# A hybrid decoder step: the samples' values stored by sample, and their new states made ahead of and between the splits of the third tile

## What is computed

```python
s_new = g_c[None, :, None, None] * s + jnp.einsum('bmhd,bmhe->bhde', kc * zeta[None, :, :, None], vc)
return s_new, o_in + o_cross
```

## Time and profile before

| | |
|---|---|
| median of 3 timed runs | 2126.41 us (2126.33 to 2126.54) |
| the profiled execution | 2127.75 us |
| its span in the profile | 2125.9 us |
| PE busy | 2101.2 us, 99% |
| DVE busy | 1449.2 us, 68% |
| ACT busy | 958.2 us, 45% |
| HBM traffic | 196 GB/s over the span |

### The profile page before, as it was taken

The page is one execution under the profiler, slowest core; times in us unless marked ns, Lnnn a source line. Parts: engine busy times, 40 slices in busy tenths (PEclk is TensorE's granted clock), DMA queues, the critical chain, the costliest instruction groups (busy, mean ns, idle before and its releaser), DMA issues.

```text
span 2125.9 us, 46489 instructions
## 1 busy us (share of the span) xinstructions
PE 2101.2 (99%) x18585; PEld 2088.5 (98%) x18585; DVE 1449.2 (68%) x2716; ACT 958.2 (45%) x1327; POOL 68.6 (3%) x94
## 2 busy tenths in 40 slices
PE   7999999999999999999999999999999999999997
PEld 7999999999999999999999999999999999999997
DVE  7888876668888667754656666565655556666665
ACT  6555633445534344443434344443434344444444
POOL 1111000000000000000000000000000000000000
PEclk9999999999999999999999999999999999999999
DMA  8666655654455566675556566665666566666653
GB/s 285 215 212 213 202 179 182 197 184 142 160 187 180 175 196 205 209 245 184 195 189 221 185 214 197 199 201 196 207 193 201 177 212 206 211 207 200 204 179 125
DMA packets 115175, 418.39 MB, mean 197 GB/s; under 512 B 13600, under 2 KB 14112, under 8 KB 114752
## 3 DMA queue, kind: packets, MB, share of 16 engines
q1 hardware_dynamic: 100800, 365.29, 53.1%
q0 software_dynamic: 9888, 34.47, 5.0%
q10 hardware_dynamic: 4320, 16.22, 2.0%
HBM read 391.55 MB, written 24.29 MB: 196 GB/s over the span
## 4 chain that ended last, share of the span: by engine, by line
PE 96%; DVE 2%; issue 1%; ACT 1%; DMA 0%; DVEq 0%; SPq 0%; ACTq 0%
PE bank L909 31%; PE bank L910 31%; PE bank L911 30%; PE bank L1082 2%; PE bank L1037 1%; DVE wlo L1161 1%; DVE s_parts L1284 0%; DVE s_new L1272 0%; ACT s_parts L664 0%; PE bank L982 0%; DVE s_rest L1279 0%; DMA acc<-xT 0%; DVE acc L1835 0%; PE bank L993 0%; PE bank L989 0%
## 5 line engine op out<-in xcount | busy, mean ns | idle before, releaser
L1161 DVE TENSOR_TENSOR wlo<-raw,whi 128x1024 fp32r<-128x1024 f32 x688 | 829.9, 1223 | 495.3 <-ACT whi L627 491.1
L627 ACT CAST whi<-raw 128x1024 fp32r<-128x1024 f32 x688 | 710.3, 1048 | 647.4 <-PE bank L911 641.7
L909 PE MATMUL bank<-xhi,whi 128*128 128x264 f32 x3200 | 911.5, 285 | 0.0
L910 PE MATMUL bank<-xlo,whi 128*128 128x264 f32 x3200 | 906.7, 283 | 0.0
L911 PE MATMUL bank<-xhi,wlo 128*128 128x264 f32 x3200 | 906.5, 283 | 0.0
L910 PEld LDWEIGHTS bank<-xlo,whi 128*128 128x128 f32 x3200 | 603.1, 188 | 0.0
L909 PEld LDWEIGHTS bank<-xhi,whi 128*128 128x128 f32 x3200 | 602.6, 188 | 0.2 <-issue 0.2
L911 PEld LDWEIGHTS bank<-xhi,wlo 128*128 128x128 f32 x3200 | 600.1, 188 | 0.0
L909 PE MATMUL bank<-xghi,whi 128*128 128x264 f32 x1152 | 333.9, 290 | 9.7 <-DVE wlo L1161 9.7
L909 PE MATMUL bank<-wexp_hi,whi 128*128 128x264 f32 x1152 | 328.0, 285 | 0.0
L910 PE MATMUL bank<-xglo,whi 128*128 128x264 f32 x1152 | 327.8, 285 | 0.0
(11 more groups left out here) (214 smaller groups left out, 1125.0 us busy)
## 6 DMA issues: line engine op xcount, KB each, us to landing
raw<-halves SPq DMA_DIRECT2D x688, 512.0 KB, 3.5
hid<-gates ACTq DMA_DIRECT2D x30, 528.0 KB, 4.8
gates<-stage POOLq DMA_DIRECT2D x17, 768.0 KB, 7.3
s_old<-ret_state POOLq DMA_DIRECT2D x8, 512.0 KB, 6.3
vs_all<-values POOLq DMA_DIRECT2D x8, 512.0 KB, 4.4
ret_sample<-s_new POOLq DMA_DIRECT2D x8, 512.0 KB, 5.2
gates<-route_mem POOLq DMA_DIRECT2D x5, 768.0 KB, 7.2
acc<-xT SPq DMA_DIRECT2D x4, 528.0 KB, 6.5
```

What stands on the lines that cost most here:

```text
L627: nc.scalar.copy(whi[:, s], raw[:, s]).then_inc(hi_done, 1)
L909: nc.tensor.matmul(out, whi[:, s, c], mh[c], start=start and c == 0, stop=False)
L910: nc.tensor.matmul(out, whi[:, s, c], ml[c], start=False, stop=False)
L1161: v.tensor_tensor(wlo[:, s], raw[:, s], whi[:, s].bitcast(F32), ALU.subtract).then_inc(lo_done, 1)
```

## The change

- `vs_all` and the DRAM scratch `values` are laid out by sample and then feature, [.., sample, e] instead of [.., e, sample]. The DVE instruction `outer` reads `vs_all` contiguously. The copy from vT into `values`, which wrote 8 neighbouring words for each partition, now writes 8 words 512 bytes apart.
- POOL: the copy of the values of head h + 1 and the broadcast back come ahead of the stores of head h. `s_new` is stored and the next `s_old` loaded before `state2` is stored, which has a semaphore of its own (`state2_ready`).
- DVE: `s_new` comes right behind `outer`, ahead of vT. Then vT, the split of half 4, `s_rest`, the split of half 5, `state2`, the last parts.
- ACT: cast of half 4, first parts of the new states, cast of half 5, `state1`, second parts.

```diff
--- before.py
+++ after.py
@@ -254,7 +254,7 @@
         v_tok = sb("v_tok", [P, 2, P], F32, mix)
         k_tok = sb("k_tok", [P, 2, P], F32, mix)
 
-        vs_all = sb("vs_all", [P, P, NSAMPLE], F32, mix)
+        vs_all = sb("vs_all", [P, NSAMPLE, P], F32, mix)
         outer = sb("outer", [P, NSAMPLE, P], F32, mix)
         scored = sb("scored", [P, 2, P], F32, mix)
         qx = sb("qx", [P, P], F32, mix)
@@ -305,7 +305,7 @@
         assert SPAN * STAGED * GB <= GROUP * T
         stages = [sb("stage", [P, SPAN, STAGED * GB])[:],
                   route_mem[:, 0:SPAN * STAGED * GB].rearrange("p (k t) -> p k t", k=SPAN)]
-        values = nc.dram_tensor("values", (P, NSAMPLE), F32).ap()
+        values = nc.dram_tensor("values", (NSAMPLE, P), F32).ap()
         gates = nc.dram_tensor("gates", (2 * QUADS, P, BLOCKS, QUAD, STAGED * GB), F32).ap()
 
 
@@ -406,6 +406,7 @@
         values_saved = sem("values_saved")
         values_in = sem("values_in")
         outer_ready = sem("outer_ready")
+        state2_ready = sem("state2_ready")
         turned = sem("turned")
         tok_ready = sem("tok_ready")
         att_ready = sem("att_ready")
@@ -566,24 +567,31 @@
             sret_out = out_sret.rearrange("b h d e -> h d b e")
             pool.dma_start(s_old[:], sret[0]).then_inc(s_in, 16)
 
-            def head(h, last):
+            def values_to_all(h):
 
                 pool.wait_ge(bank_free[0], h + 1)
-                pool.dma_start(values, vT[:, NPROMPT:T]).then_inc(values_saved, 16)
+                pool.dma_start(values.rearrange("b e -> e b"), vT[:, NPROMPT:T], allow_slow_non_contiguous=True)\
+                    .then_inc(values_saved, 16)
                 pool.wait_ge(values_saved, 16 * h + 16)
                 if h:
                     pool.wait_ge(outer_ready, h)
-                pool.dma_start(vs_all[:].rearrange("p e b -> p (e b)"),
-                               values.rearrange("e b -> (e b)").unsqueeze(0).to_broadcast([P, P * NSAMPLE]))\
+                pool.dma_start(vs_all[:].rearrange("p b e -> p (b e)"),
+                               values.rearrange("b e -> (b e)").unsqueeze(0).to_broadcast([P, P * NSAMPLE]))\
                     .then_inc(values_in, 16)
+
+            def states_out(h):
                 pool.wait_ge(snew_ready, 2 * h + 2)
+                pool.dma_start(sret_out[h], s_new[:]).then_inc(st_stored, 16)
+                if h < HEADS - 1:
+                    pool.dma_start(s_old[:], sret[h + 1]).then_inc(s_in, 16)
+                pool.wait_ge(state2_ready, h + 1)
                 pool.dma_start(out_pret[h], state2[:]).then_inc(st_stored, 16)
-                pool.dma_start(sret_out[h], s_new[:]).then_inc(st_stored, 16)
-                if not last:
-                    pool.dma_start(s_old[:], sret[h + 1]).then_inc(s_in, 16)
-
+
+            values_to_all(0)
             for h in range(HEADS):
-                head(h, h == HEADS - 1)
+                if h < HEADS - 1:
+                    values_to_all(h + 1)
+                states_out(h)
             pool.wait_ge(y_ready, 2 * HEADS)
             pool.dma_start(out_conv, conv_out[:]).then_inc(conv_stored, 16)
             pool.wait_ge(conv_stored, 16)
@@ -656,12 +664,12 @@
 
                 nc.scalar.activation(warm[:, n + 1:n + 2], warm[:, 0:1], ACT.Abs_reciprocal_sqrt)
 
-            def state_parts(p):
-                for sem_, of, need, done in ((snew_ready, s_new, 0, s_part1), (s_rest1, s_rest, 1, s_part2)):
-                    for t in range(2):
-                        act.wait_ge(sem_, 2 * p + t + 1)
-                        some = slice(4 * t, 4 * t + 4)
-                        nc.scalar.copy(s_parts[:, need, some], of[:, some]).then_inc(done, 1)
+            def state_part(p, n):
+                sem_, of, done = ((snew_ready, s_new, s_part1), (s_rest1, s_rest, s_part2))[n]
+                for t in range(2):
+                    act.wait_ge(sem_, 2 * p + t + 1)
+                    some = slice(4 * t, 4 * t + 4)
+                    nc.scalar.copy(s_parts[:, n, some], of[:, some]).then_inc(done, 1)
 
             def swap(k):
 
@@ -720,11 +728,15 @@
                 if norm:
                     root(h)
                 if loads_tiles(h) and not first:
-                    ahead(r, 1)
+                    hi_half(r, 4)
+                if att:
+                    state_part(h - 1, 0)
+                if loads_tiles(h) and not first:
+                    hi_half(r, 5)
                 if att:
                     act.wait_ge(st_done, h)
                     nc.scalar.copy(state1[:], bank[7][:, 0:P]).then_inc(s1_ready, 1)
-                    state_parts(h - 1)
+                    state_part(h - 1, 1)
                 if tiles:
                     tile_done(r, 1)
                     if not first:
@@ -1255,29 +1267,36 @@
 
             def outer_products(p):
                 dve.wait_ge(values_in, p * 16 + 16)
-                v.tensor_tensor(outer[:], vs_all[:].rearrange("p e b -> p b e"),
+                v.tensor_tensor(outer[:], vs_all[:],
                                 kT[:, NPROMPT:T].unsqueeze(2).to_broadcast([P, NSAMPLE, P]), ALU.mult)\
                     .then_inc(outer_ready, 1)
 
             def new_states(p):
-                dve.wait_ge(st_done, p + 1)
-                dve.wait_ge(s1_ready, p + 1)
+
+                dve.wait_ge(s_in, (p + 1) * 16)
+                dve.wait_ge(outer_ready, p + 1)
                 if not (isinstance(p, int) and p == 0):
                     dve.wait_ge(st_stored, p * 32)
-                v.scalar_tensor_tensor(out=state2[:], in0=state1[:], scalar=of_head("gchunk", p),
-                                       in1=bank[7][:, P:2 * P], op0=ALU.mult, op1=ALU.add)
-                dve.wait_ge(s_in, (p + 1) * 16)
-                dve.wait_ge(outer_ready, p + 1)
                 for t in range(2):
                     v.scalar_tensor_tensor(
                         out=s_new[:, 4 * t:4 * t + 4, :], in0=s_old[:, 4 * t:4 * t + 4, :],
                         scalar=of_head("gone", p), in1=outer[:, 4 * t:4 * t + 4, :],
                         op0=ALU.mult, op1=ALU.add).then_inc(snew_ready, 1)
+
+            def state_rests(p):
                 for t in range(2):
                     some = slice(4 * t, 4 * t + 4)
                     dve.wait_ge(s_part1, 2 * p + t + 1)
                     v.tensor_tensor(s_rest[:, some], s_new[:, some], s_parts[:, 0, some], ALU.subtract)\
                         .then_inc(s_rest1, 1)
+
+            def second_state(p):
+                dve.wait_ge(st_done, p + 1)
+                dve.wait_ge(s1_ready, p + 1)
+                v.scalar_tensor_tensor(out=state2[:], in0=state1[:], scalar=of_head("gchunk", p),
+                                       in1=bank[7][:, P:2 * P], op0=ALU.mult, op1=ALU.add).then_inc(state2_ready, 1)
+
+            def state_lasts(p):
                 for t in range(2):
                     some = slice(4 * t, 4 * t + 4)
                     dve.wait_ge(s_part2, 2 * p + t + 1)
@@ -1343,12 +1362,18 @@
                 if att:
                     attention_in(h - 1)
                     outer_products(h - 1)
+                    new_states(h - 1)
                 if tiles and not first:
                     values_out(h)
                 if loads_tiles(h) and not first:
-                    ahead(r, 1)
+                    lo_half(r, 4)
                 if att:
-                    new_states(h - 1)
+                    state_rests(h - 1)
+                if loads_tiles(h) and not first:
+                    lo_half(r, 5)
+                if att:
+                    second_state(h - 1)
+                    state_lasts(h - 1)
                 if loads_tiles(h) and not first:
                     ahead(r, 2)
                 if att:
```

## The result

The changed kernel takes 2136.32 us in the median (2135.25 to 2138.0, 6 runs), the kernel before 2126.78 us (2126.33 to 2127.18, 6 runs): the ratio is 1.0046, with a 95% interval of 1.0035 to 1.0056. It is 9.5 us slower, where 2123.5 us had been forecast. The profiled execution has a span of 2134.3 us, 8.4 more than before.

The account below looks back on a forecast made before the run. PE bounds the kernel, losing time only waiting for `s_parts`. Gains of 2.64 us (loop) and 0.94 (first block) less 0.65 (first copy) give 2.9; 2127.75 - 2.9 - 1.34 (profiled to median) = 2123.5 us, range 2122.5 to 2127.0.

Parts of the forecast that it names:

- What bounds the kernel, and what the waits are worth: PE, 99% busy; its repeating waits for `s_parts` cost 2.64 us in six loop heads, 0.94 in the first block.
- ceiling: PE's waits for `s_parts` at L982: 3.58 us together, the most the edits could gain.
- Part 1 (a): DVE's `outer`, reading `vs_all` contiguously: 1.2 us instead of 2.19, repeated operand taken as free.
- Part 1 (b): Copy of vT to DRAM in 1024 pieces of 4 B: 5.2 us, taken from the store of `s_new`.
- Part 1 (c): Broadcast of the values back: same rows and bytes, 4.4 us, so no change.
- Parts 2 and 3: DVE's new order brings `s_parts` 1.0 us early in a loop head; ACT's new order costs 0.
- Part 4: POOL's new order: cost 0 in loop heads, over 10 us to spare; 0.65 us in the first head.
- Rival (A): Slower 4 B copy, paid once in the first head, one us per us beyond 5.2; chance 0.17, for 6 to 12 us.
- Rival (B): Slower in all heads: `s_old`, queued behind the copy, comes late from 17 us of copy; 20 us gives 2150; chance 0.08.
- Slower by more needs a copy of over 12 us: Times above the range's 2127.0 us: only by (B) and the end of (A), chance 0.09.

Follow-up runs that it names:

- the order alone: Kernel before with only the new order on POOL, DVE and ACT; layout, copy, broadcast and `outer` as before: 2123.87 us against 2126.9, ratio 0.9986.
- the run at a pitch of 32 B: Changed kernel, 4 B pieces stored at a pitch of 32 B, broadcast reading constants instead (real values left out): 2122.46 us against 2126.66, ratio 0.998.
- the run with late values: Order alone, 32 B pieces throughout, three spare copies waited for ahead of the first head's copy: 2134.14 us against 2126.48 of the kernel before, ratio 1.0037.
- the run with the first head alone: Order alone, with only the first head's values in 4 B pieces and contiguous `outer`: 2133.55 us against 2126.8 of the kernel before, ratio 1.0031.

## Why the prediction was wrong

- **What bounds the kernel, and what the waits are worth:** right in kind. Taking the waits away gained 3.0 us with the order alone and 4.2 us with the 4 B pieces apart. The 4.2 is over the "ceiling" of 3.58: the last block, which served as the measure of no wait, still had 0.14 us of one. L982 followed L975 by 0.36 us there and follows by 0.22 in the run at a pitch of 32 B. That is 8 x 0.14 = 1.1 us that no row of waits showed. 3.58 + 1.1 is 4.7, and the profiles bear it out: 191.12 - 187.59 = 3.5 us from the first L982 to the last, and 1.1 in the first block. The 4.2 of the medians lies within its interval (2.1 to 6.2 us) of that.
- **Part 1 (a), `outer` at 1.2 us:** right, 1.218 in the median, with its repeated operand, where a `wlo` of the same 1024 columns takes 1.219.
- **Part 1 (b), the copy at 5.2 us:** the step that failed. It took 9.9 us in the first head and 10.2 to 12.3 in the others, from issue to the issue of the broadcast. The row taken as nearest, `s_new` with its 1024 pieces, was near in a quantity that costs little: at a pitch of 32 B the same 1024 pieces let the broadcast go after 3.2 to 5.3 us, against 2.0 to 2.9 for the 128 pieces of 32 B in the order alone. What the two transfers didn't share was how densely small pieces lie in DRAM.
- **Part 1 (c), the broadcast "nothing":** wrong. 8.0 us instead of 4.4, as it runs together with all the weights that the copy had held up. In the median over the heads 1.4 of these 3.6 us show with the new order alone (5.8).
- **Parts 2 and 3, the order on DVE and ACT:** right in the loop. With the order alone the stretch from the first L982 to the last shrinks from 191.12 to 188.54 us: 2.58, where 2.64 were forecast. But the margin wasn't there in every head: with `outer` as slow as before, `s_parts` was to come early in all of them, and L993 stands 0.46 to 0.68 us behind L986 in three. The 0.94 of the first block doesn't come from the order: PE still waits 0.8 there.
- **Part 4, POOL:** the time to spare in the loop was nearly enough: worked out for 5.2 us, it stood 10.2 to 12.3 us at a cost of 1.0 us for all seven copies, where "Cost 0" was forecast. The first head's slack of 2.35 us was right too, and the copy overran it by 9.9 - 4.55 = 5.3, the broadcast by 3.6 more: 8.9, the length of the wait of `outer`.
- **Rival (A)** had the place and the mechanism, a late first head, but only the copy in its price: with 9.9 us it gives 2123.5 + 4.7 = 2128.2. Two terms were missing: the broadcast's 3.6 us and the clock after the idle PE, 2.2 us in the run with late values. 2128.2 + 3.6 + 2.2 = 2134.0, near the 2133.6 of the run with the first head alone; with the loop's 1.0 it is 2135.0, and 1.3 of the measured 2136.3 stay open. The range ended at 2127.0, a copy of 8.7 us by this rival's own price, because the row of `s_new` had made slower ones look unlikely. The chances didn't follow that price: "Slower by more needs a copy of over 12 us" should have read 8.7, and by its own terms, (B) and half of (A), the chance of it was about 0.17 and not 0.09.
- **Rival (B)** didn't come: `s_old` was never what `new_states` waited for. It waited once, 0.5 us, for a store that stands behind it in POOL's queue, that of `state2` (`ret_prompt`). The Trainium skill's rule that a strided last dimension should be made contiguous (DMA: Bandwidth & Descriptors, Rules for kernel authors) pointed the right way, and this trace agrees: the one such copy is what lost the time. The reason that stands with the rule, one descriptor for each element, isn't the one that the runs bear out: 1024 pieces of 4 B landed in 4.7 us at a pitch of 32 B.

## What to carry to other kernels

Price a transfer that has no row by how its pieces lie at the target, not by how many there are: small pieces side by side are another case than the same pieces apart. A transfer that nobody waits for can still stop those that somebody does, so look at the rate of all transfers while it runs. And where the pipeline starts there is no slack yet: a step that a loop hides almost for nothing is paid in full in the first iteration, and once more in the clock if the bounding engine stands idle.

## What the runs showed of the hardware

- 1024 writes of 4 B that lie side by side in DRAM bring the transfers of the whole core down to 22 to 30 GB/s, some 10 us long for 4 KB (the changed kernel). The same 1024 pieces at a pitch of 32 or 64 B land in 4.7 to 4.8 us behind a broadcast, with the weights at 4.4 us as ever. Eight pieces of one partition side by side were slow too (2145 us, one run). Whether sharing 32 B or crowding into 4 KB is what counts wasn't separated, and writes into SBUF weren't tried.
- In the changed kernel the granted clock fell to 0.50 at 53 us, with PE idle since 49.2, and came back to 1.00 at 63 us, with PE busy again since 58.66. In the run with late values the same cost 2.2 us beside the wait of 8.1.
